# A column one-hot table in bf16 in the gate stage, and 34 early expert blocks in place of 36

## The reference, cut to what matters

```
def peer_ffn(h, peer_wq, sub_keys1, sub_keys2, peer_u, peer_v):
    ...                                    # q1, q2: two query halves per head
    s1 = jnp.einsum('bthd,nd->bthn', q1, sub_keys1, ...)
    s2 = jnp.einsum('bthd,nd->bthn', q2, sub_keys2, ...)
    v1, i1 = lax.top_k(s1, PEER_TOPK)      # 16 best of 128 keys
    v2, i2 = lax.top_k(s2, PEER_TOPK)
    cand_s = v1[..., :, None] + v2[..., None, :]
    cand_i = i1[..., :, None] * N_KEYS + i2[..., None, :]
    top_s, pos = lax.top_k(cand_s, PEER_TOPK)
    eid = take_along_axis(cand_i, pos)     # 8 heads x 16 experts per token
    gate = jax.nn.softmax(top_s, axis=-1)
    a = gelu(einsum('td,tkd->tk', h, peer_u[eid]))
    return einsum('tk,tkd->td', gate * a, peer_v[eid])
```

## Time and profile before

| what | us |
|---|---|
| median of three runs (960.44 to 962.30) | 960.62 |
| the profiled execution, whole | 962.64 |
| its span in the trace | 960.8 |
| PE busy | 950.7 (99%) |
| DVE busy | 765.0 (80%) |
| ACT busy | 476.5 (50%) |
| POOL busy | 210.0 (22%) |
| granted PE clock in the gate rounds | 1.00 (the 2.4 GHz level) |
| stage: start to the first gate round | 0 to 242.6 |
| stage: gate rounds | 242.6 to 350.7 |
| stage: early part of the expert blocks | 353.7 to about 447 |
| stage: late blocks | to the end |

### The profile page before, as it was taken

The page is one execution under the profiler, slowest core; times in us unless marked ns, Lnnn a source line. Parts: engine busy times, 40 slices in busy tenths (PEclk is TensorE's granted clock), DMA queues, the critical chain, the costliest instruction groups (busy, mean ns, idle before and its releaser), DMA issues.

```text
span 960.8 us, 16339 instructions
## 1 busy us (share of the span) xinstructions
PE 950.7 (99%) x5324; PEld 827.5 (86%) x5324; DVE 765.0 (80%) x1454; ACT 476.5 (50%) x846; POOL 210.0 (22%) x249
## 2 busy tenths in 40 slices
PE   9999999999999999999999999999999999999998
PEld 9998899898888888888888888888888888888887
DVE  5899759899999998888676776777777777777776
ACT  6576554433888874334334434434444444444442
POOL 3075238887777740000000000000000000000000
PEclk9999999999999999999999999999999999999999
DMA  9544138826443458777555555555555555555554
GB/s 289 155 132 132 45 109 292 214 57 208 147 130 118 137 178 264 241 236 237 176 190 202 175 196 197 178 197 192 179 202 187 179 206 183 181 210 177 187 206 153
DMA packets 73593, 174.72 MB, mean 182 GB/s; under 512 B 6208, under 2 KB 39104, under 8 KB 73296
## 3 DMA queue, kind: packets, MB, share of 16 engines
q1 hardware_dynamic: 73120, 172.02, 53.4%
q0 software_dynamic: 288, 2.10, 1.1%
q10 hardware_dynamic: 144, 0.08, 0.0%
HBM read 165.26 MB, written 6.82 MB: 179 GB/s over the span
## 4 chain that ended last, share of the span: by engine, by line
PE 77%; DVE 1%; issue 0%; ACT 0%; DVEq 0%; ACTq 0%
PE psum L1964 36%; PE psum L1944 17%; PE psum L1829 10%; PE psum L1947 9%; PE psum L1907 3%; PE psum L1529 0%; DVE big L1329 0%; DVE big L1123 0%; DVE big L1119 0%; DVE big L1158 0%; DVE big L1150 0%; DVE big L1131 0%; PE psum L1895 0%; ACT gel L689 0%; DVE big L1147 0%
## 5 line engine op out<-in xcount | busy, mean ns | idle before, releaser
L1964 PE MATMUL psum<-rr 128*128 128x512 f32 x1536 | 366.0, 391 | 0.1
L1964 PEld LDWEIGHTS psum<-rr 128*128 128x128 f32 x1536 | 287.4, 188 | 60.0 <-issue 0.2
L1944 PE MATMUL psum<-h_all,rr 128*128 128x512 f32 x728 | 260.6, 392 | 0.0
L785 ACT ACTIVATE rr<-raw 128x1024 fp32r<-128x1024 f32 x94 | 99.7, 1061 | 235.5 <-PE psum L1964 234.5
L1247 DVE TENSOR_TENSOR rr<-raw,rr 128x1024 fp32r<-128x1024 f32 x94 | 115.2, 1225 | 123.1 <-ACT rr L785 123.1
L1947 PE MATMUL psum<-h_all,rr 128*128 128x256 f32 x728 | 188.7, 280 | 0.0
L1944 PEld LDWEIGHTS psum<-h_all,rr 128*128 128x128 f32 x728 | 136.6, 188 | 27.2 <-DVE rr L1163 0.3
L1947 PEld LDWEIGHTS psum<-h_all,rr 128*128 128x128 f32 x728 | 136.7, 188 | 7.1
L1829 PE MATMUL psum<-t32s,raw 128*128 128x256 f32 x576 | 131.8, 379 | 1.5 <-ACT gel L689 1.0
L683 ACT ACTIVATE rr<-raw 128x1024 fp32r<-128x1024 f32 x91 | 96.6, 1062 | 50.2 <-DMA raw<-in_peer_u_dram 48.7
L1829 PEld LDWEIGHTS psum<-t32s,raw 128*128 128x128 f32 x576 | 106.1, 190 | 15.0 <-issue 1.6
(11 more groups left out here) (213 smaller groups left out, 1137.4 us busy)
## 6 DMA issues: line engine op xcount, KB each, us to landing
raw<-in_peer_v_dram SPq DMA_DIRECT2D x128, 512.0 KB, 3.6
raw<-in_peer_u_dram SPq DMA_DIRECT2D x127, 512.0 KB, 4.0
big<-in_w_in_dram SPq DMA_DIRECT2D x10, 1024.0 KB, 5.4
big<-in_peer_wq_dram SPq DMA_DIRECT2D x8, 1024.0 KB, 6.9
up_kept<-gel SPq DMA_DIRECT2D x36, 128.0 KB, 2.1
gel<-up_kept SPq DMA_DIRECT2D x34, 128.0 KB, 4.0
big<-in_w_out_dram SPq DMA_DIRECT2D x4, 1024.0 KB, 5.4
rr<-big POOLq DMA_DIRECT2D x2, 1024.0 KB, 11.5
```

The lines of the kernel that those rows point to most:

```text
L785: act.activation(v_sp[s][:, 0, :], v_raw[s], ACT.Copy).then_inc(v_hi, 1)
L1944: return pe.matmul(both, ut[s][:, 0, k, :], ht[:, :, k, :], start=(k == 0), stop=(k == DK - 1))
L1964: i = pe.matmul(psum[:, 4 + 2 * t + n, :], g_sp[:, s, x, t * P:(t + 1) * P], v_sp[s][:, y, n * 512:(n + 1) * 512], start=(first and m == 0 ...
```

## The change

Seven edits.

1. `EARLY` is 34 instead of 36. Blocks 34 and 35 move from the early to the late form, and `fill_end` spreads two blocks less over the gate rounds. The ring of buffers is turned accordingly.
2. The column one-hots are bf16 and lie with the token innermost (`p s n q`: number, then eight tokens). They are compared with `pick16`, the column numbers in bf16, against a table `numbers_in` that fills PSUM bank 0 with every number eight times in bf16. Both buffers together now take 1024 words of `raw` (3D to 4D) instead of 2048.
3. The row one-hots have the output of before, but read the same table, every eighth element.
4. ACT and POOL read a token's column one-hot as every eighth bf16 element, 16 bytes apart.
5. ACT builds the table in two steps: 1024 bf16 elements into SBUF (ahead of an early gelu), then a copy of 512 words to PSUM. It copies the column numbers out first, then the row numbers.
6. SP no longer waits for the rounds before it loads `v_2`.
7. At the start, three fp32 matmuls that keep PE busy become five of type fp32r on a tile that POOL sets to one.

```
-EARLY, EARLY_TOP = 36, 14
+EARLY, EARLY_TOP = 34, 14
...
-        cols = raw[:, 2 * D:4 * D].rearrange("p (s q n) -> p s q n", s=2, q=GRP)
+        cols = raw[:, 3 * D:4 * D].bitcast(BF16).rearrange("p (s n q) -> p s n q", s=2, q=GRP)
+        pick16 = picks[:, 1, 0:SEQ // 2].bitcast(BF16)
+        numbers_sb = big[:, xs_at:xs_at + NK * GRP // 2]
...
-        iota_in = psum[:, 0, 0:NK]
+        numbers_in = psum[:, 0, :].bitcast(BF16).rearrange("p (n q) -> p n q", q=GRP)
...
                     load_v(1)
-                    sp.wait_ge(ohg_up, NQ - 1)
-                    sp.wait_ge(ohp_up, NQ - 1)
                     load_v(2)
...
             numbers(PH - 1)
+            act.activation(numbers_sb.bitcast(BF16).rearrange("p (n q) -> p n q", q=GRP), iota.unsqueeze(2).to_broadcast([P, NK, GRP]),
+                           ACT.Copy).then_inc(a_iota, 1)
             for e in range(PH - 2, EARLY_TOP - 3):
                 early_gelu(e)
-            act.activation(iota_in, iota, ACT.Copy).then_inc(a_iota, 1)
+            act.wait_ge(a_iota, 1)
+            act.activation(psum[:, 0, :], numbers_sb, ACT.Copy).then_inc(a_iota, 1)
...
-            act.activation(picks[:, 0:2, :].rearrange("p a t -> p (a t)"), psum[:, 6, :], ACT.Copy).then_inc(pk_ev, 1)
+            act.activation(pick16, psum[:, 6, SEQ:2 * SEQ], ACT.Copy).then_inc(pk_ev, 1)
+            act.activation(picks[:, 0, :], psum[:, 6, 0:SEQ], ACT.Copy).then_inc(pk_ev, 1)
...
-                        i = act.activation(pairs_at[q % 2][:, j, part, :], cols[:, q % 2, j, :], ACT.Copy, scale=scale)
+                        i = act.activation(pairs_at[q % 2][:, j, part, :], cols[:, q % 2, :, j], ACT.Copy, scale=scale)
...
-            def ones(out, a, tok, n):
-                dve.tensor_tensor(out, iota_in.unsqueeze(1).to_broadcast([P, n, NK]),
-                                  picks[:, a, tok:tok + n].unsqueeze(2).to_broadcast([P, n, NK]), ALU.is_equal).then_inc(oh_up, 1)
+            def ones_cols(q):
+                dve.tensor_tensor(cols[:, q % 2], numbers_in, pick16[:, GRP * q:GRP * (q + 1)].unsqueeze(1).to_broadcast([P, NK, GRP]),
+                                  ALU.is_equal).then_inc(oh_up, 1)
+
+            def ones_rows(q):
+                dve.tensor_tensor(rows_at[q % RS], numbers_in.rearrange("p n q -> p q n"),
+                                  picks[:, 0, GRP * q:GRP * (q + 1)].unsqueeze(2).to_broadcast([P, GRP, NK]), ALU.is_equal).then_inc(oh_up, 1)
...
-                    i = pool.tensor_tensor(pairs_at[q % 2][:, 0:n, part, :], cols[:, q % 2, 0:n, :],
+                    i = pool.tensor_tensor(pairs_at[q % 2][:, 0:n, part, :], cols[:, q % 2, :, 0:n].rearrange("p n q -> p q n"),
                                            p.unsqueeze(2).to_broadcast([P, n, NK]), ALU.mult)
...
-            stay_awake(3)
+            pe.wait_ge(p_ones, 2)
+            stay_awake_r(5)
```

More of the change, by code:

```diff
@@ L188, in layer @@
         half = take(1)
+        ones_r = rr[:, 8 * D:8 * D + P]
         eps = take(1)
@@ L765, in keep_high @@
                 act.activation(gates[:, :, HALF * c:HALF * c + HALF], half_sums(c, 0), ACT.Copy).then_inc(b_ev, 1)
-            act.wait_ge(pk_ev, 2)
+            act.wait_ge(pk_ev, 3)
             for q in range(NQ):
@@ L1224, in _ @@
             dve.tensor_tensor(ut[0][:, 1], u_first, f(ut[0][:, 0]), ALU.subtract).then_inc(ut_lo, 1)
-            dve.wait_ge(a_iota, 1)
+            dve.wait_ge(a_iota, 2)
             dve.wait_ge(pk_ev, 1)
@@ L1230, in _ @@
                     dve.wait_ge(ohp_up, q - 1)
-                ones(cols[:, q % 2], 1, GRP * q, GRP)
+                ones_cols(q)
                 if q == 0:
-                    dve.wait_ge(pk_ev, 2)
+                    dve.wait_ge(pk_ev, 3)
                     dve.tensor_tensor(picks[:, 2, :].rearrange("p (a k m) -> p a k m", a=2, k=DK),
@@ L1238, in _ @@
                     dve.wait_ge(b_done, 2 * (q - RS + 1))
-                ones(rows_at[q % RS], 0, GRP * q, GRP)
+                ones_rows(q)
                 if q:
@@ L1335, in _ @@
             pool.memset(ones_t, 1.0).then_inc(p_ones, 1)
+            pool.memset(f(ones_r), 1.0).then_inc(p_ones, 1)
             pool.memset(half, -0.5).then_inc(p_half, 1)
@@ L1500, in gated @@
                         pool.wait_ge(d_plo, 1)
-                    i = pool.tensor_tensor(pairs_at[q % 2][:, 0:n, part, :], cols[:, q % 2, 0:n, :],
+                    i = pool.tensor_tensor(pairs_at[q % 2][:, 0:n, part, :], cols[:, q % 2, :, 0:n].rearrange("p n q -> p q n"),
                                            p.unsqueeze(2).to_broadcast([P, n, NK]), ALU.mult)
                 i.then_inc(ohp_up, 1)
-            pool.wait_ge(pk_ev, 2)
+            pool.wait_ge(pk_ev, 3)
             for q in range(NQ):
@@ L1573, in stay_awake, with stay_awake_r @@
                     pe.matmul(psum[:, 6, 0:P], ones_t, ones_t, start=True, stop=True)
+            def stay_awake_r(n):
+                for _ in range(n):
+                    pe.matmul(psum[:, 6, 0:P], ones_r, ones_r, start=True, stop=True)
             def high_first(c, t):
@@ L1840, in early_ready @@
                 if e == FILL0 + 1:
-                    pe.wait_ge(pk_ev, 2)
+                    pe.wait_ge(pk_ev, 3)
                     pe.wait_ge(d_plo, 1)
```

## The result

The changed kernel takes 984.58 us (median of four, 982.97 to 986.47) against 960.53 before; the ratio is 1.0243, 95% interval [1.0223, 1.0263]. The forecast was 958.5, the range ended at 971.5: the change is 24 us slower, not slightly faster. The profiled execution took 983.13 us, its span is 981.3.

What follows compares the result with a forecast made beforehand. The prediction took DVE to bound the gate rounds (3.45 us), PE close behind and bounding afterwards. Its terms, -8.6 for the rounds, +5.6 for two blocks and +0.9 for the table, gave -2.1 us: 958.5 us, range 956.7 to 971.5.

Steps and rivals of the forecast that it cites:

- The strided reads of POOL and ACT: ACT and POOL reading column one-hots 16 bytes apart: taken at no cost, high end 1.55 times; called the weakest choice.
- The ACT rival: Strided reads slow ACT's six multiplications, 0.46 us more in its loop, round 3.63, time 972.7; chance 0.10.
- The prediction's high end: Strided reads by ACT and POOL cost 1.55 times, the ratio of DVE's 64-byte-step reduction to its row compares.
- The POOL rival: Strided reads slow POOL's gate-round instructions (L1511): 959.4 at the low reading, 968.7 midway, 977.4 high; chance 0.18.
- the 1.58 from which it would decide: Gate rounds: POOL's pair of instructions becomes the round once one takes over 1.58 us, against 1.22 now.
- The compare: DVE's column compare in the gate rounds: about 0.7 us in bf16 from PSUM, DVE's round down 0.5 to 2.95.
- The rival by which a source in PSUM keeps it at 1.21: Column compare stays at one element per cycle, DVE holds the round at 3.45, time 967.1; chance 0.12.
- The loop model: Gate rounds: ACT's loop with PE is longest at 3.17 us, against 3.449 before, giving -8.6 us over 31 rounds.
- PE's own share by the formula: PE in a gate round: 10.06 fill instructions at 0.216 us plus 0.96 for eight gate matmuls, 3.13 us.
- The two blocks: Two early blocks become late, each costing 2.80 us more: +5.6 us.
- The table: ACT builds it ahead of an early gelu for which PE waits: 1.05 less a slack of 0.13, +0.9 us.
- The start: Five fp32r matmuls replace three fp32 at the start: taken at nothing, ends -0.3 and +0.4 us.

Runs made afterwards that it cites:

- the 38-block kernel: Changed kernel with bf16 column one-hots token by token, column numbers written twice each, and 38 early blocks instead of 34: 961.2 us, 1.0004 to the kernel before.
- the last layout: Changed kernel with bf16 one-hots token by token, column numbers written twice: 961.8 us with 34 early blocks, 959.0 with 36, 961.2 with 38.

## Why the prediction was wrong

- **The failed step: "The strided reads of POOL and ACT", with "For the forecast I take no cost".** The reason given was that both engines are slower than DVE per element and may hide a slower fetch. For ACT its own rows speak against it: 1024 elements in 1.06 us, where DVE's compare of as many took 1.21. And nothing was hidden, on POOL either. ACT's instruction went from 0.396 to 0.522 us and the distance from one to the next from 0.29 to 0.42: 1.0 ns more for each element.
- **The ACT rival named the place and the mechanism, and was mis-sized.** It added 6 x 0.077 = 0.46 us to ACT's loop, from DVE's 0.60 ns. Measured is 6 x 0.125 = 0.75, and 3.17 + 0.75 = 3.92 against 3.93 in the trace. With that price the prediction's own sum is 31 x (3.92 - 3.449) + 6.5 = +21.1, 981.7 us; the two spans differ by 20.5. The prediction's high end, 1.55 times, would have covered it: 0.29 x 1.55 = 0.45 us from one to the next, measured 0.42. But only POOL's case was worked out at both ends, ACT's at 0.60 ns alone. By the high end ACT's loop is 3.17 + 6 x 0.16 = 4.13 us, and the time 960.62 + 31 x 0.68 + 6.5 = 988. The case got 0.10, and already at 972.7 it lay outside the range.
- **The POOL rival**: 0.48 ns an element instead of 0.60, so its instructions are 1.52 us apart, under the 1.58 from which it would decide. It pays, but it holds nothing while ACT is slower: relieving it alone won nothing. The threshold itself is too simple. With ACT relieved, POOL's instructions at 1.57 us, under that threshold, still brought the round from 3.19 to 3.28, though POOL waited 11.9 us for DVE in the stage; which chain of waits closes there was not followed. The Trainium skill's rule ("GPSIMD Engine Reference", section "Performance pitfalls for Q7 kernels") gave half as long again per element; the trace shows a quarter (1.256 to 1.561) at 16 bytes, and about 1% at 8. That the cost sets in above 8 bytes agrees with these runs.
- **The compare was right**: 0.681 us where 0.7 was taken. The rival by which a source in PSUM keeps it at 1.21 fell. The Trainium skill's tier table ("VectorE: DVE Perf Modes", section "The perf-mode tier table") is not borne out for this operation; its section "Why PSUM operands drop a tier" is. The row compare at its 16-byte step out of PSUM cost nothing: 1.215 us.
- **The loop model was right**: 3.17 us was computed, and 3.19 is measured where both engines read side by side (962.0 us in all). But PE's own share by the formula is 3.13, so near that this round does not test the two apart; the round of the changed kernel, 3.92 by ACT's loop and 3.93 measured, does.
- **The two blocks**: +5.6 said, 6.0 (34 blocks in the kernel before) and 6.7 (the two traces) measured. The distance of sums was right (507.9 / 92 = 5.52). About 0.8 us of the 6.7 is at the stage's end, where the last half of the gates now waits for ACT (PE's down products start 4.93 us after the last group, before 4.17). The table: +0.7 in PE's wait (below) for 0.9 said, but this wait differs between kernels that have the same table: 1.0 to 1.6 us in the four traces without it, 1.6 to 2.95 in the six with it. The start: nothing, as said.

```profile
218.59 3.69 PE L1845 MATMUL psum<-t32s,raw 128*128 128x256 f32 x16 [1.70 <-ACT gel L690]
```

- **Also off**: with the reads free the changed kernel takes 962.0 us, 0.4 more than the kernel before beside it, where the sum said 2.1 less. Of these 2.5 us about 1 is the blocks and 0.5 the 0.02 us in each round. The rest was not taken apart; five of its ten executions have the lower mean clock told of below, and its profiled one has PE idle for 2.16 us at 452.3, behind a load of u that came late, which the trace of before has not. So even without the step the change would have been worth nothing that could be told from noise.

## What to carry to other kernels

A layout that makes one engine's compare packed can make its readers strided; price every reader, by a row or a run of its own engine, before the writer's gain is booked. Then look for a layout that keeps both, as the one with the numbers written twice does. An engine with 12 of 14 us busy is not far from the path when its work closes a loop with PE: ACT had 0.28 us of room in a round of 3.45, and six instructions of 0.125 us more broke it. And look first at how far the next engine is behind the one that you relieve: here PE stood 0.07 us behind DVE (0.09 by the prediction's formula), and the best version gained 2.3 us though the compare fell from 1.21 to 0.68.

## What the runs showed of the hardware that was not expected

- ACT reading SBUF in 2-byte or 4-byte elements 16 bytes apart: 0.52 us for 128 elements, against 0.39 side by side and 0.40 at 8 bytes. DVE's two-source compare kept its fast rate with bf16 from PSUM in runs of eight, four and two elements (0.680 to 0.682 us for 1024).
- A short wait of PE can cost twice. In the profiled execution of the 38-block kernel a load of u came late. The rows are ACT waiting for it, PE waiting in turn, then stretches of 1 us, with these columns: the length, the busy us of PE, of its weight loads, of DVE, ACT and POOL, the granted clock, the DMA share and GB/s:

```profile
473.65 1.06 ACT L684 ACTIVATE rr<-raw 128x1024 fp32r<-128x1024 f32 x1 [3.56 <-DMA raw<-in_peer_u_dram]
```
```profile
476.02 0.50 PE L1960 MATMUL psum<-h_all,rr 128*128 128x512 f32 x1 [1.88 <-DVE rr L1167]
```
```profile
475.00:476.00 1.00, 0.00 (x0) 0.00 (x0) 1.00 (x2) 0.66 (x1) 0.00 (x0) 1.00 0.48 193
476.00:477.00 1.00, 0.98 (x5) 0.89 (x6) 1.00 (x2) 0.39 (x2) 0.00 (x0) 1.00 0.01 4
477.00:478.00 1.00, 1.00 (x5) 0.86 (x5) 1.00 (x2) 0.94 (x1) 0.00 (x0) 0.64 0.00 0
478.00:479.00 1.00, 1.00 (x4) 0.81 (x4) 0.93 (x4) 0.00 (x0) 0.00 (x0) 0.50 0.68 61
479.00:480.00 1.00, 1.00 (x5) 0.90 (x5) 0.96 (x1) 0.00 (x0) 0.00 (x0) 0.50 0.41 147
480.00:481.00 1.00, 1.00 (x5) 0.76 (x4) 0.47 (x1) 0.00 (x0) 0.00 (x0) 0.66 1.00 410
481.00:482.00 1.00, 1.00 (x6) 0.82 (x5) 0.23 (x1) 0.00 (x0) 0.00 (x0) 1.00 0.97 397
```

  PE stood still for 1.88 us, and over 1 us after it worked again the clock fell from the 2.4 to the 1.2 GHz level for about 3.4 us, 1.7 us of work lost. Together that is 3.6 us: this execution took 963.42, the shortest of that kernel 959.86. The profiled execution of the kernel with POOL alone relieved (986.44 us, shortest 982.76) shows the same at the table: PE is idle for 2.95 us until 220.03, then the lower level stands from 220.6 to 224.0.

  The length of the wait alone does not decide it. In the profiled execution of the kernel before with only the new start, PE was idle for 2.77 us and the clock stayed at the upper level:

```profile
468.56 0.50 PE L1952 MATMUL psum<-h_all,rr 128*128 128x512 f32 x1 [2.77 <-DVE rr L1164]
```
```profile
469.00:476.00 7.00, 7.00 (x39) 6.00 (x38) 4.45 (x8) 2.67 (x4) 0.00 (x0) 1.00 0.40 150
```

  Nor did the clock fall after 1.70 us of idle time in the changed kernel, 2.10 in the one with 36 blocks, 2.12 and 2.16 with both engines relieved, or 2.14 and 2.19 at the step of 8 bytes. A fall of 3.4 us takes 0.002 from an execution's mean clock, so the 0.998 of unprofiled executions points to one such fall: four of ten with 34 early blocks in the last layout, one of ten with 36, three of ten with 38. Why such a wait comes in some executions and not in others, and what lets the clock fall after one and not after another, stays open.
